# The first output projection on split operands: three rounded products for each float32 product, high parts on ScalarE, low parts on GpSimd and VectorE

## What is computed

```python
y_a = rwkv7_mix(...)                      # (yn + bonus) * gate @ w_a
y_b = dilated_attention_mix(...)          # o @ w_b
merged = sigmoid(p_ga) * y_a + sigmoid(p_gb) * y_b
x = x + gate_m[:, None, :] * rms_norm(merged @ w_out[i], g_post_mix[i])
h = modulate(rms_norm(x, g_pre_ffn[i]), shift_f, scale_f)
u, gt = jnp.split(h @ w_ffn_in[i], 2, axis=-1)
```

## Time and profile before

| | us |
|---|---|
| median of 3 runs | 1661.06 (1656.12 to 1663.27) |
| profiled execution | 1660.98 |
| its span, first to last instruction | 1659.2 |
| TensorE busy / VectorE / ScalarE / GpSimd | 1590.4 / 1132.3 / 727.6 / 284.9 |
| granted TensorE clock, mean over the span | 0.994 |

### The profile page before, as it was taken

The page is one execution under the profiler, slowest core; times in us unless marked ns, Lnnn a source line. Parts: engine busy times, 40 slices in busy tenths (PEclk is TensorE's granted clock), DMA queues, the critical chain, the costliest instruction groups (busy, mean ns, idle before and its releaser), DMA issues.

```text
span 1659.2 us, 29366 instructions
## 1 busy us (share of the span) xinstructions
PE 1590.4 (96%) x11682; PEld 1369.1 (83%) x11682; DVE 1132.3 (68%) x1816; ACT 727.6 (44%) x1071; POOL 284.9 (17%) x332
## 2 busy tenths in 40 slices
PE   3999988999999999999999999999999999999998
PEld 3998777785888888888896888888888888698887
DVE  5886445375788877787657568875878666755554
ACT  3444423412444454444447444435444355744443
POOL 0441344121500100000016000000000002500000
PEclk9999989999999999999999999999999999999999
DMA  9863110267788838886640488875787563164531
GB/s 391 333 256 127 52 53 4 71 239 271 268 316 318 330 125 334 323 311 245 225 172 1 163 324 335 305 282 213 304 335 300 235 200 116 56 234 161 227 152 64
DMA packets 59540, 363.83 MB, mean 219 GB/s; under 512 B 14000, under 2 KB 14768, under 8 KB 39472
## 3 DMA queue, kind: packets, MB, share of 16 engines
q1 hardware_dynamic: 59440, 362.42, 57.5%
HBM read 361.32 MB, written 1.08 MB: 218 GB/s over the span
## 4 chain that ended last, share of the span: by engine, by line
PE 84%; DVE 7%; issue 3%; DMA 2%; ACT 2%; POOL 1%; SPq 0%; POOLq 0%; DVEq 0%; ACTq 0%
PE psum L896 20%; PE psum L900 10%; PE psum L915 5%; PE psum L916 5%; PE psum L914 5%; PE psum L858 4%; PE psum L967 2%; PE psum L1068 2%; PE psum L1004 2%; PE psum L1005 2%; PE psum L1006 2%; DMA arena<-in_ada_head 2%; PE psum L1356 1%; PE psum L1357 1%; PE psum L1358 1%
## 5 line engine op out<-in xcount | busy, mean ns | idle before, releaser
L896 PE MATMUL psum<-split 128*128 128x512 f32 x1440 | 392.4, 394 | 0.0
L2018 DVE TENSOR_TENSOR split<-ring,split 128x2048 fp32r<-128x2048 f32 x100 | 229.4, 2298 | 174.0 <-ACT split L1563 169.6
L896 PEld LDWEIGHTS psum<-split 128*128 128x128 f32 x1440 | 248.9, 189 | 35.3
L1563 ACT ACTIVATE split<-ring 128x2048 fp32r<-128x2048 f32 x100 | 190.4, 1909 | 182.9 <-PE psum L900 96.3
L900 PEld LDWEIGHTS psum<-split 128*128 128x128 f32 x1440 | 220.7, 189 | 30.5
L900 PE MATMUL psum<-split 128*128 128x256 f32 x1440 | 228.9, 281 | 0.0
L2700 POOL TENSOR_TENSOR scratch<-scratch 128x512 f32<-128x512 f32 x45 | 58.4, 1298 | 773.4 <-ACT scratch L1588 773.4
L1987 DVE CUSTOM_DVE_ANT_0 arena<-arena,c_row 128x1024 f32<-128x1024 f32 x144 | 167.6, 1220 | 0.0
L916 PE MATMUL psum<-split 128*128 128x512 f32 x400 | 156.5, 391 | 0.0
L915 PE MATMUL psum<-split 128*128 128x512 f32 x400 | 156.5, 391 | 0.0
L914 PE MATMUL psum<-split 128*128 128x512 f32 x400 | 155.9, 390 | 0.0
(11 more groups left out here) (455 smaller groups left out, 3219.6 us busy)
## 6 DMA issues: line engine op xcount, KB each, us to landing
ring<-in_up SPq DMA_DIRECT2D x55, 2048.0 KB, 10.5
arena<-in_ada SPq DMA_DIRECT2D x168, 512.0 KB, 6.5
ring_down<-in_down SPq DMA_DIRECT2D x55, 1024.0 KB, 4.9
ring<-in_in SPq DMA_DIRECT2D x19, 2048.0 KB, 8.9
ring<-in_gates SPq DMA_DIRECT2D x4, 2048.0 KB, 8.9
arena<-in_ada_head SPq DMA_DIRECT2D x4, 1536.0 KB, 18.6
ring_down<-in_w_out SPq DMA_DIRECT2D x3, 2048.0 KB, 12.3
ring<-in_w_out SPq DMA_DIRECT2D x3, 2048.0 KB, 8.8
```

The costliest lines, as they stand in the source:

```text
L896: mm(bank[4 + j], up_hi[:, h, a], h_both[:, kt_].rearrange("p s n -> p (s n)"), start=(kt_ == 0), stop=(kt_ == KD - 1), skip_group_check=True)
L1563: F(up_hi[:, h], ring[:, (g + c) % 2, h * 2048:(h + 1) * 2048], ACT.Copy).then_inc(up_high, 1)
L2018: tt(up_lo[:, h], ring[:, (g + c) % 2, h * 2048:(h + 1) * 2048], up_hi[:, h].bitcast(F32), ALU.subtract).then_inc(up_low, 1)
```

## The change

`project` becomes `project_first`, with three products for each term. The halves of `w_out` change places: the first column half is now in `side`, the second in the ring, whose slot is then freed by the fourth bank instead of the third. ScalarE makes the high parts of both halves and of `merged`. GpSimd makes the first half's low parts in place; VectorE makes those of `merged` (in place) and of the second half. The transposes of the next norm move from the end of the third bank to behind three terms of the fourth. In the hand-over behind it, `low_half` and `high_half` of the first token half move behind the residual add of the second. Two semaphores of the second mixer (`cs_sub`, `cs_prob`) become one, with the same waits.

```diff
+        first_hi = [[split[:, a:a + 512] for a in (6656, 7168, 7680, 4096, 4608, 8192, 8704, 9216)],
+                    [split[:, a:a + 512] for a in range(0, 4096, 512)]]
+        first_raw = [side, ring[:, (G_GATES + 7) % 2]]
+        first_lo = [ring_down_split[:], ring_split[:, (G_GATES + 7) % 2]]
+        merged_hi, merged_lo = split[:, 12288:14336], split[:, 14336:16384]
...
-            sp.dma_start(side, T["w_out"][1]).then_inc(side_loaded, 16)
+            sp.dma_start(side, T["w_out"][0]).then_inc(side_loaded, 16)
...
-            load(g + 7, T["w_out"][0], (bank_full, 3))
+            load(g + 7, T["w_out"][1], (bank_full, 4))
...
+            def project_first(n):
+
                 for t in range(NT):
+                    for h in range(2):
                         for k in range(KD):
+                            if t == 0:
+                                if h == 0:
+                                    pe.wait_ge(w_low, 37 + k + 1)
+                                    pe.wait_ge(first_low, k + 1)
+                                else:
+                                    pe.wait_ge(w_low, 37 + KD + k + 1)
+                            if t == 1 and h == 1 and k == 3:
+                                transposes(n, 0)
+                            a, w = slice(k * S + t * P, k * S + (t + 1) * P), slice(k * 512, (k + 1) * 512)
+                            mm(bank[2 * t + h], merged_hi[:, a], first_hi[h][k], start=(k == 0), stop=False, skip_group_check=True)
+                            mm(bank[2 * t + h], merged_hi[:, a], first_lo[h][:, w], start=False, stop=False, skip_group_check=True)
+                            last = mm(bank[2 * t + h], merged_lo[:, a], first_hi[h][k], start=False, stop=(k == KD - 1), skip_group_check=True)
                         last.then_inc(bank_full, 1)
...
@@ ScalarE, norm_halves: high_half(0) behind output_root(n - 1, 1) @@
...
-            channel_major(TG, CM_G, 0, range(9, 16))
+            channel_major(TG, CM_G, 0, range(9, 14))
+            for j in (14, 15):
+                channel_major(TG, CM_G, 0, (j,))
+                for k in ((0, 1), (2, 3, 4))[j - 14]:
+                    high_first(0, k)
+            act.wait_ge(gn_ready, PAIRS)
+            for k in range(5, KD):
+                high_first(0, k)
+            for j in range(8):
+                act.wait_ge(ym_ready, j + 1)
+                f(merged_hi[:, j * S:(j + 1) * S], merged[:, j * S:(j + 1) * S], ACT.Copy).then_inc(w_high, 1)
+            for k in range(KD):
+                high_first(1, k)
...
@@ VectorE, hand_over_normed: low_half(n + 1, 0) behind normed_added(n, 1) @@
...
+            def low_merged(j):
+
+                c = slice(j * S, (j + 1) * S)
+                dve.wait_ge(w_high, 37 + KD + j + 1)
+                tt(merged_lo[:, c], merged[:, c], merged_hi[:, c].bitcast(F32), ALU.subtract).then_inc(w_low, 1)
...
                         tt(ytmp[:, n % 2], bank[4 + n % 2][:, 0:S], sig[:, j * S:(j + 1) * S], ALU.mult).then_inc(ym_read, 1)
+                        if j:
+                            low_merged(j - 1)
                         ada_late(19 + j)
+                low_merged(7)
+                for k in range(KD):
+                    c = slice(k * 512, (k + 1) * 512)
+                    dve.wait_ge(w_high, 37 + 2 * KD + k + 1)
+                    tt(first_lo[1][:, c], first_raw[1][:, c], first_hi[1][k].bitcast(F32), ALU.subtract).then_inc(w_low, 1)
...
@@ GpSimd, behind rwkv() and ahead of the adds of the merge @@
+            for k in range(KD):
+                c = slice(k * 512, (k + 1) * 512)
+                pool.wait_ge(w_high, 37 + k + 1)
+                tt(first_lo[0][:, c], first_raw[0][:, c], first_hi[0][k].bitcast(F32), ALU.subtract).then_inc(first_low, 1)
```

More of the change, by code:

```diff
@@ L562, in build @@
         cs_full = sem("cs_full")
-        cs_sub = sem("cs_sub")
+        cs_dve = sem("cs_dve")
         cs_exp = sem("cs_exp")
-        cs_prob = sem("cs_prob")
         cst_full = sem("cst_full")
@@ L577, in build @@
         o_ready = sem("o_ready")
+        first_low = sem("first_low")
         def up_slot(g):
@@ L618, in low_at, with high_at @@
         def low_at(l, p):
-            return 37 + (PIECES2 + OUT_PIECES + 1) * l + 2 + p
+            return 53 + (PIECES2 + OUT_PIECES + 1) * l + 2 + p
+        def high_at(l, p):
+            return low_at(l, p) + KD
         DONE_MIX1, DONE_FFN1, DONE_A, DONE_MIX2, DONE_B, PER_LAYER_DONE = 0, 4, 7, 10, 14, 10
@@ L1055, in project_split @@
                             transposes(n, 0)
-            def project(g, lhs, sides, ready, base, n, begun=0):
-                w0 = chunk(g)
-                pe.wait_ge(side_loaded, 16 * sides)
+            def project_first(n):
                 for t in range(NT):
-                    for h, w in enumerate((w0, side)):
+                    for h in range(2):
                         for k in range(KD):
[L1064 to L1068, removed]
+                            if t == 0:
[10 more added lines that the diff above has]
+                            last = mm(bank[2 * t + h], merged_lo[:, a], first_hi[h][k], start=False, stop=(k == KD - 1), skip_group_check=True)
                         last.then_inc(bank_full, 1)
-                        if t == 1 and h == 0:
-                            transposes(n, 0)
             def early_gate(j, terms=range(KD)):
@@ L1504, in mixer2 @@
                 tiles_of(13)
-                pe.wait_ge(cs_prob, l + 1)
+                pe.wait_ge(cs_dve, 2 * l + 2)
                 for t in range(NT):
@@ L1541, in _ @@
             merge()
-            project(G_GATES + 7, lambda k, t: merged[:, k * S + t * P:k * S + (t + 1) * P], 1, ym_ready, 0, 1)
+            project_first(1)
             ffn_split(0, 1, G_FFN1)
@@ L1632, in norm_halves @@
                             output_root(n - 1, 1)
-                            if downs is not None:
-                                high_half(0)
+                            high_half(0)
                         else:
@@ L1881, in mixer2 @@
                     high_piece2(j + 7)
-                act.wait_ge(cs_sub, l + 1)
+                act.wait_ge(cs_dve, 2 * l + 1)
                 f(csm, csm, ACT.Exp, scale=SCALE).then_inc(cs_exp, 1)
@@ L1957, in _, with high_first @@
             f(c_late, c_late, ACT.Silu).then_inc(c_ready, 1)
-            channel_major(TG, CM_G, 0, range(9, 16))
+            def high_first(h, k):
+                if k == 0 and h == 0:
+                    act.wait_ge(side_loaded, 16)
+                elif k == 0:
+                    act.wait_ge(slot_full[(G_GATES + 7) % 2], full_count(G_GATES + 7))
+                f(first_hi[h][k], first_raw[h][:, k * 512:(k + 1) * 512], ACT.Copy).then_inc(w_high, 1)
+            channel_major(TG, CM_G, 0, range(9, 14))
[11 more added lines that the diff above has]
+                high_first(1, k)
             act.wait_ge(ym_full, 16)
@@ L2134, in hand_over_normed @@
                     modulate_half(n + 1, sub, 0)
-                    low_half(n + 1, 0)
                     gated(n, 3)
@@ L2142, in hand_over_normed @@
                 normed_added(n, 1)
-                if not late:
-                    low_half(n + 1, 0)
+                low_half(n + 1, 0)
                 mean_square(n + 1, 1)
@@ L2517, in mixer2 @@
                 v.settle()
-                tt(csm3, csm3, cst[:, 48:64].unsqueeze(2).broadcast_to([P, 16, 16]), ALU.mult).then_inc(cs_prob, 1)
+                tt(csm3, csm3, cst[:, 48:64].unsqueeze(2).broadcast_to([P, 16, 16]), ALU.mult).then_inc(cs_dve, 1)
                 def maxima(i):
```

9 lines of the change are left out of this document (4 added, 5 removed).

## The result

The changed kernel takes 1671.3 us (median of 6 runs, 1669.19 to 1675.45) against 1661.47 before (6 runs): 9.8 us more. The ratio taken over the runs is 1.0064, a little above that of the two medians, with an interval of 1.0051 to 1.0076. That is slower by over 0.5%, and the interval is far narrower than the 0.5% that I took for what a measurement can tell. The forecast of 1668.7 was 2.6 us too low; the time lies just inside my range (to 1671.5), but beyond the 0.5% within which I had put most of the chance. The profiled execution took 1672.64 us with a span of 1670.8, 11.66 more than that of before.

A forecast was written before the change was run, and what follows sets the result against it. TensorE was taken to bound most of the span, with VectorE setting the time ahead of the merge. 5.3 + 1.7 + 0 + 0.7 = 7.7 us on 1660.98 gave 1668.7 us; range 1659.5 to 1671.5.

The forecast's parts named there:

- GpSimd in the group norm: Ahead of the merge, five GpSimd low parts alternate with VectorE's steps and delay the norm's end by 5.3 us.
- Rival 1: GpSimd gets in between VectorE's group-norm steps never or too seldom to matter: 1661.7 us, chance 0.22.
- rival 3: Worse: GpSimd's rounding form is half as fast, or the second FFN chunk stalls `up(1)`: 1671 to 1674 us, chance 0.13.
- The clock: At the merge's restart, TensorE's granted clock falls after over 5 us of idle: 1.7 us, bounds 0 and 1.7.
- Projection and hand-over: From projection to `up(0)`: the 7.6 us saved at best are lost to VectorE's queue behind row 26, net 0.
- rival 2: GpSimd does not delay the norm and row 26 is there when VectorE asks for it: 1656.3 us, chance 0.10.
- The low half: In the hand-over, the moved `low_half` makes the second half's transposes 0.7 us late; bounds 0 and 1.2.
- a stall for the second FFN chunk: In the first FFN, the chunk's later release is covered by `up(0)`: at most 2 us, taken as none.
- the first two stalls: TensorE's idle ahead of the merge, over 5 us, and ahead of the moved transposes, 4 to 5; clock 1.7 each.

The follow-up runs named there:

- e9: Changed kernel, with each of GpSimd's low parts cut into two instructions of 256 columns: 1673.7 us.
- e10: Changed kernel, with each of GpSimd's low parts cut into four instructions of 128 columns: 1666.5 us.
- e3: Changed kernel, with the first FFN's gate row written ahead of the load of its chunk 1 instead of behind it and the down chunks: 1668.0 us.
- e8: e5 with the transposes of the first token half back behind the third bank: 1663.85 us.
- e1: Changed kernel, with GpSimd's eight low parts held until the whole group norm is done; ScalarE's high parts stay: 1659.84 us.
- e6: e5 with VectorE taking the last low part of `merged` and two weight low parts ahead of rows 26 and 27: 1656.93 us.
- e7: e6 with the low half of the first token half moved behind the modulation of the second: 1657.45 us.
- e4: Kernel before, with only the projection weight half's ring slot released by the fourth bank instead of the third: 1662.45 us.
- e2: Changed kernel, with GpSimd's low parts 0 and 1 left early and parts 2 to 7 held until the group norm is done: 1663.77 us.
- e5: Changed kernel with the edits of e1 and e3 together: 1660.32 us.

## Why the prediction came out low

**GpSimd in the group norm (5.3).** Right in place and mechanism, a little too large: it was 4.9. The 2.1 ns a column, read off one product of 1536 columns, is confirmed at 128, 256 and 512 by e9 and e10; what was left out is that 0.13 us of each instruction do not hold. Rival 1 falls with the rows of 1.37. The rounding form is no slower to speak of (1.34 to 1.37 beside VectorE, against 1.29), so that half of rival 3 falls too. The Trainium skill, page "SBUF — State Buffer", section "SBUF: two separate sides", has the other engine blocked for a whole instruction; the trace agrees that the two take turns, one step for one part, but the hold is 0.95 us of an instruction of 1.34, and 0.14 of one of 0.47 (13.24/28): the measurement decides.

**The clock (1.7).** It fell, for 2.45 us, beyond the 1.7 that I had put as the upper bound. The price came from a return after 1.94 us of idle, and falls of that kind do cost 1.7 in these runs; this idle was 4.96 us, and behind such long ones the cost was 2.4 to 2.8 (e3, e8 and e9 too). e1 gave back both terms with one wait.

**Projection and hand-over (0).** Nearly right, -0.4 by the marks (+7.35 at the start of the projection, +6.97 at `up(0)`), and for the reasons given, so that rival 2 falls: row 26's late transfer, the low parts behind it, rows 30 and 31 behind those. e6 shows this by moving the last low part of `merged` and two of the weights' ahead of row 26, and row 27 ahead of the other six: 3.5 us. In detail two misses offset each other: TensorE waited 1.60 us at its first bank, not 1, and 3.46 at the transposes, not 4 to 5. The 379.05 at which I let TensorE start is the end of its last record; e1 starts 0.35 before that.

**The low half (0.7).** 0.5, by T less U and by e7. It cannot simply go back to its old place, since it writes where the second half's high parts lie, which the fourth bank still reads; e7 puts it later instead.

**The step that failed** is the one clause "a stall for the second FFN chunk, which is now released by the fourth bank instead of the third: [...] at most 2 us. I take none." I set the load of that chunk against `up(0)`, found it covered, and stopped. What stands behind it in SP's queue I did not follow: two `down` loads, the gate row's write, SP's wait for it, and only then the load of chunk 2. The cost was 3.75 us by the marks, 1.94 of idle and 1.72 of clock behind it; e3 takes it away by moving the row alone (3.3 us in the medians), e4 makes the idle time with one line in the kernel before. My bound of 2 us would have held for the idle time; the clock behind it I had counted for the first two stalls and not for this one. Rival 3 named a stall by the second chunk and 1671 to 1674 us, which is where the time came out, with another chunk and by another way than I gave for it.

The sum by the marks: 4.9 + 2.45 - 0.4 + 0.5 + 3.75 = 11.2. Without the failed step it is 7.5, close to the forecast's 7.7, and that is partly luck: 0.75 too little for the clock against 1.0 too much in the three other terms together. The profiled executions lie 11.66 apart: ahead of the dot product the kernel after is 0.97 us shorter, and behind N it is 1.35 us longer. The stretch ahead of the dot product differs by up to 2.7 us between these profiles. Behind N the two kernels without the change (before and e4) take 1060.7 and 1060.8 us, the ten with it 1061.1 to 1062.9; whether the one semaphore in place of two costs something there, no run isolates. Nor have I traced why the medians lie only 9.8 apart.

## What to carry to other kernels

When a transfer is released later, walk the whole queue behind it to the next wait of the issuing engine: a 4 KB write behind 4 MB of loads can set the time where the loads themselves are covered. A helper engine that looks free still holds VectorE for about 2.1 ns a column while VectorE is on the path; start it where VectorE reads an operand from PSUM or nothing waits for it, or, failing that, cut its instructions to about the length of VectorE's steps (quarters of 0.47 us left 1.7 us of delay, halves of 0.80 left 4.3). And put work that waits for nothing ahead of a dot product that waits for its transfer: this order was worth 3.5 us here, and without it the cheaper products gained next to nothing.

## What the runs showed of the hardware

- A VectorE step with one tensor read from SBUF and two per-partition scalars (the TENSOR_SCALAR at 351.97, 1.35 us instead of 0.40) is held by GpSimd as much as those with two. Steps that read one tensor from PSUM and one from SBUF are not: 0.42 us beside GpSimd's low parts in e1.
- VectorE and GpSimd hold each other. In the merge of the kernel before, GpSimd's adds of 256 columns start 0.16 us behind VectorE's dot products and take 1.64 us, the dot products 1.22. After, the `low_merged` steps stand in between, the adds start 0.17 us ahead of the dot products and take 0.83, and the dot products 1.75.
- How long TensorE idles does not alone decide whether the granted clock falls. Of the idle stretches in these profiles, 1.59 (e6), 1.75 (e4), 1.93 (e10, `up(2)`) and 3.00 us (e1, transposes) left it at 1.00, while 1.80 (e2, first bank), 1.94, 1.94 (after, `up(2)`), 2.1 (e2, merge) and 3.12 us (e5, transposes) brought it down to 0.50 for a time. Why, these runs leave open. A fall behind 1.8 to 3.7 us of idle cost 1.7 us, one behind 4.4 to 5.0 us cost 2.4 to 2.8.
